# Half-width Fourier products, the full call's norms inside the context call, and a decay step without GpSimd, in a two-layer SSD, Fourier and mixture-of-experts block

## The reference, cut to what matters

```python
def _token_mixer(u, uc, ...):
    pc = uc @ w_in
    yc, s_f, s_b = _bidir_ssd(xsc, dtc, a, bmc, cmc, s0, s0)     # context first
    p = u @ w_in
    y, _, _ = _bidir_ssd(xs, dt, a, bm, cm, s_f, s_b)            # then the latents
    def merge(proj, z_, x_, y_):
        y_ = (y_ + x_ * d).reshape(b_, l_, D_INNER)
        ssm = _gated_rms_norm(y_, z_, norm_w) @ w_br_ssm
        four = _fourier_mix(proj[..., OFF_FOUR:OFF_GATE]) @ w_br_four
        gates = sigmoid(proj[..., OFF_GATE:])
        return (gates[..., :D] * ssm + gates[..., D:] * four) @ w_out

def _fourier_mix(t):            # 4 groups of 256 features, 256 tokens
    f = fft2(t.reshape(1, 256, 4, 256), axes=(1, 3), norm='ortho').real

def _ssd(...):                  # chunks of 128 tokens, 24 heads in 4 groups of 6
    seg = acum[:, :, :, None] - acum[:, :, None, :]
    lmat = exp(where(tri, seg, -inf))
    y_diag = einsum('bclsg,bclsgr,bcsgrp->bclgrp', scores, lmat, xdt)
```

## Time and profile before

| | |
|---|---|
| median of 3 runs | 2913.14 us (2911.34 to 2913.22) |
| the profiled execution: its own time, its span | 2910.98 us, 2909.1 us |
| busy: TensorE, VectorE, ScalarE, GpSimd | 2614.9, 996.8, 496.0, 345.5 us |
| calls 0 and 1 of the mixer end, experts of layer 0 | about 860 us, to about 1640 us |
| call 2 | 1684.7 to 1798 us |
| call 3 | 1798 to about 2190 us |
| experts of layer 1 | to the end |
| from the first to the last `y_products` of calls 0, 1, 3 | 71.87, 77.19, 77.20 us |

### The profile page before, as it was taken

One profiled execution on the slowest core, in us unless ns is written; L12 is line 12 of the kernel. 1 busy time (PEld: TensorE's weight loads), 2 busy tenths in 40 slices (PEclk: granted clock), 3 DMA queues, 4 the chain that ended last, 5 costly groups with the idle time before them and its releaser, 6 DMA issues. The chain is left out here.

```text
span 2909.1 us, 35099 instructions
## 1 busy us (share of the span) xinstructions
PE 2614.9 (90%) x11348; PEld 1644.3 (57%) x11348; DVE 996.8 (34%) x2285; ACT 496.0 (17%) x964; POOL 345.5 (12%) x448
## 2 busy tenths in 40 slices
PE   6999999999997899999999886999997799999994
PEld 4876788877884333433443374877786343343431
DVE  1334914528357111111111575342914411111114
ACT  1222311323221111111111022132211011111110
POOL 0001300003001111212111000000300211121110
PEclk8999999999999999999999987999998899999997
DMA  8762543435333999999999841763433599999993
GB/s 298 238 210 82 161 137 119 160 98 163 104 131 150 392 409 403 410 408 404 409 407 386 308 133 44 250 230 106 156 116 105 223 407 384 394 402 391 382 366 139
DMA packets 293117, 742.93 MB, mean 255 GB/s; under 512 B 33176, under 2 KB 207904, under 8 KB 238240
## 3 DMA queue, kind: packets, MB, share of 16 engines
q1 hardware_dynamic: 264672, 666.11, 60.7%
q0 software_dynamic: 28352, 75.56, 6.7%
HBM read 735.12 MB, written 52.58 MB: 271 GB/s over the span
## 5 line engine op out<-in xcount | busy, mean ns | idle before, releaser
L712 PE MATMUL psum<-arena 128*128 128x256 f32 x1984 | 452.0, 389 | 18.0 <-ACT arena L1167 12.1
L1070 PE MATMUL psum<-arena 128*64 128x512 f32 x1472 | 363.5, 639 | 77.5 <-DMA arena<-in_w 77.3
L712 PEld LDWEIGHTS psum<-arena 128*128 128x128 f32 x1984 | 384.2, 196 | 73.7 <-ACT arena L1167 13.1
L945 PE MATMUL psum<-arena 128*128 128x512 f32 x832 | 374.3, 594 | 0.0
L1913 DVE COPY arena<-psum 128x512 f32<-128x512 f32 x92 | 63.6, 691 | 614.4 <-PE psum L957 310.3
L1070 PEld LDWEIGHTS psum<-arena 128*64 128x64 f32 x1472 | 113.8, 145 | 261.0 <-issue 255.5
L945 PEld LDWEIGHTS psum<-arena 128*128 128x128 f32 x832 | 152.1, 192 | 154.4 <-issue 154.4
L1370 ACT ACTIVATE arena<-psum 128x512 f32<-128x512 f32 x92 | 55.0, 598 | 1053.1 <-PE psum L957 589.2
L720 PE MATMUL psum<-arena 128*128 128x256 f32 (+1 forms) x1088 | 229.6, 373 | 5.0 <-ACT arena L1167 5.0
L720 PEld LDWEIGHTS psum<-arena 128*128 128x128 f32 x1088 | 201.0, 196 | 31.3 <-ACT arena L1167 5.2
L957 PE MATMUL psum<-arena 128*128 128x512 f32 x416 | 197.3, 618 | 5.8 <-DVE arena L1727 3.6
(11 more groups left out here) (302 smaller groups left out, 2597.6 us busy)
## 6 DMA issues: line engine op xcount, KB each, us to landing
arena<-in_w SPq DMA_DIRECT2D x414, 1024.0 KB, 13.2
arena<-in_w_in SPq DMA_DIRECT2D x92, 1024.0 KB, 5.1
arena<-in_w_ada SPq DMA_DIRECT2D x32, 1024.0 KB, 7.6
arena<-results POOLq DMA_DIRECT2D x12, 2048.0 KB, 10.0
arena<-in_w_br_ssm SPq DMA_DIRECT2D x24, 768.0 KB, 4.4
arena<-in_w_ada SPq DMA_DIRECT2D x8, 2048.0 KB, 14.8
arena<-cumulated SPq DMA_DIRECT2D x36, 384.0 KB, 3.9
arena<-in_w_br_four SPq DMA_DIRECT2D x12, 1024.0 KB, 5.0
```

Source lines behind the costliest of these rows:

```text
L712: last = mm(o[:, a, :], w[:, k, a * P:(a + 1) * P], rhs[:, k, :], start=first and k == 0, stop=final and k == ks - 1, skip_group_check=True)
L945: last = mm(o.rearrange("p (a n) -> p a n", a=2), lhs(k), w[:, k, :, :], start=k == 0, stop=k == KD - 1)
L1070: last = mm(bank[0][c, :].rearrange("p (a n) -> p a n", a=2), xTe[0][:, k, c], w13[b][:, k, :, :], start=k == 0, stop=k == KD - 1)
```

## The change

`FH` is 129, `TH` is 127 and `AHEAD`, the call that is prepared early, is 3.

1. **Half-width Fourier products.** The inputs are real, so the spectrum's second half mirrors the first. `feature_dft` now has 258 columns (129 cosines, 127 sines between two zero columns) instead of 512, with four banks (3 to 6) instead of two. `token_dft` has, for each of two feature tiles, two products of 129 columns and two of 127 instead of four of 256, into bank 7 (bank 3 for the last group). VectorE's new `unfold` takes the place of ScalarE's copy: a copy of 4 columns, a copy of 254 and four additions or subtractions of 127, two of them written backwards. The rows of `w_br_four` come in the order that this leaves. `token_dft` of groups 1 and 2 waits for the `unfold` before it. The first feature product stands ahead of the waits for the states and the modulation.
2. **Norms of the full call among the context call's.** Call 3's norms are made in call 2, after slabs xbc 3 and 4, its transposes and copies after slabs 5 and 6, into buffers that call 2 leaves free. Call 2's state products move behind the four "four" slabs of call 3, four each.
3. **No GpSimd in the decay.** The forward segments are made by ScalarE: six `Relu` and six `Exp` of 128 by 128 with a bias column each. VectorE keeps the backward ones, and makes both multiplications and the addition; `weigh(it)` now stands after `tail(it - 1)` and `head(it)` before it.

```diff
-    dft = np.zeros((2, SEQ, 2 * SEQ), np.float32)
+    dft = np.zeros((2, SEQ, 2 * FH), np.float32)
+    dft[0, :, 0:FH] = np.cos(ang[:, 0:FH])
+    dft[0, :, FH + 1:2 * FH - 1] = np.sin(ang[:, 1:FH - 1])
+    dft[1, :, 0:FH] = np.cos(ang[:, 0:FH]) / SEQ
+    dft[1, :, FH:FH + TH] = np.sin(ang[:, 1:FH - 1]) / SEQ
...
+        uT_of, mT_of, lnx_of = [uT, uT, uT, mT], [mT, mT, mT, uT], [lnx, lnx, lnx, zs_row]
...
+                    if m != AHEAD:
+                        for t in range(NT):
+                            u_transposes(m, t)
...
                             channel_major("four", j, uT, KD)
                             late_ada("four", j)
+                            if m == AHEAD:
+                                state_products(m - 1, False, 4 * j, 4 * j + 4)
...
+                        if m == AHEAD - 1 and j >= 5 and j < 7:
+                            u_transposes(AHEAD, j - 5)
...
-                    if not full:
-                        state_products(0, 16)
...
                         def feature_dft(g):
-                            if g >= 1:
-                                pe.wait_ge(t_f1c.sem, t_f1c.at(m, g))
+                            if g >= 2:
+                                pe.wait_ge(t_f1c.sem, t_f1c.at(m, g - 1))
...
                         def token_dft(g):
                             pe.wait_ge(t_f1c.sem, t_f1c.at(m, g + 1))
-                            if g >= 1:
+                            if 1 <= g < GROUPS - 1:
                                 pe.wait_ge(t_f2c.sem, t_f2c.at(m, g))
+                            o = bank[7 if g < GROUPS - 1 else 3]
                             for a in range(2):
-                                for i, (t, part) in enumerate([(t, part) for t in range(NT) for part in range(2)]):
-                                    last = mm(bank[6][:, a * SEQ:(a + 1) * SEQ],
...
+                                for at, n, src, c0 in ((a * FH, FH, a, 0), (2 * FH + a * TH, TH, FH + a, FH)):
+                                    for t in range(NT):
+                                        last = mm(o[:, at:at + n], fA[:, g % 2, t, src:src + P], dft[:, 1, t, c0:c0 + n], start=t == 0, stop=t == 1)
...
+                        def decay(it):
+                            c, h0 = it // GROUPS, (it % GROUPS) * HPG
+                            f, v = seg[it % 2]
+                            act.wait_ge(t_rin[it % 2].sem, t_rin[it % 2].at(m, 32 * (it // 2 + 1)))
+                            for r in range(HPG):
+                                i_ = a_(f[:, r, :], f[:, r, :], ACT.Relu, scale=-1.0, bias=acu[:, c, h0 + r:h0 + r + 1])
+                            link(i_)
+                            act.wait_ge(t_seg.sem, t_seg.at(m, it + 1))
                             a_(v, v, ACT.Exp).then_inc(t_exp.sem, 1)
+                            for r in range(HPG):
+                                i_ = a_(f[:, r, :], f[:, r, :], ACT.Exp, scale=-1.0, bias=log_dt[:, c, h0 + r:h0 + r + 1])
+                            i_.then_inc(t_exp.sem, 1)
...
+                        if m == AHEAD - 1 and j >= 3 and j < 5:
+                            norm(lnx_of[AHEAD][:, j - 3, :], xres[:, TILES[CALLS[AHEAD][1]][j - 3], :], t_lnx.sem)
...
+                            f, v = seg[it % 2]
+                            sm = smask[it % 2]
+                            link(V.tensor_tensor(v, v, sm[:, 1, :].unsqueeze(1).to_broadcast([P, HPG, P]), ALU.mult))
+                            dve.wait_ge(t_exp.sem, t_exp.at(m, 2 * it + 2))
+                            link(V.tensor_tensor(f, f, sm[:, 0, :].unsqueeze(1).to_broadcast([P, HPG, P]), ALU.mult))
+                            V.tensor_tensor(f, f, v, ALU.add).then_inc(t_lm.sem, 1)
...
+                        def unfold(g):
+                            dve.wait_ge(t_f2.sem, t_f2.at(m, g + 1))
+                            o = bank[7 if g < GROUPS - 1 else 3]
+                            cos_ = o[:, 0:2 * FH].rearrange("p (a t) -> p a t", a=2)
+                            sin_ = o[:, 2 * FH:2 * FH + 2 * TH].rearrange("p (a t) -> p a t", a=2)
+                            V.tensor_copy(fO[:, 2 * g:2 * g + 2, 0:SEQ:P], cos_[:, :, 0:FH:P])
+                            half = ytmp[:, g % 2, 0:2 * TH].rearrange("p (a t) -> p a t", a=2)
+                            link(V.tensor_copy(half, sin_))
+                            for a in range(2):
+                                f_ = fO[:, 2 * g + a, :]
+                                V.tensor_tensor(f_[:, 1:P], cos_[:, a, 1:P], half[:, a, :], ALU.add if a else ALU.subtract)
+                                last = V.tensor_tensor(f_[:, SEQ - 1:P:-1], cos_[:, a, 1:P], half[:, a, :], ALU.subtract if a else ALU.add)
+                            last.then_inc(t_f2c.sem, 1)
...
+                        unfold(0)
+                        unfold(1)
                         head(0)
+                        unfold(2)
+                        unfold(3)
                         weigh(0)
-                        for it in range(8):
-                            if it:
-                                tail(it - 1)
-                            if it % 2 == 0 and it:
+                        for it in range(1, 8):
+                            head(it)
+                            tail(it - 1)
+                            if it % 2 == 0:
                                 merge_four(it // 2 - 1)
-                            if it < 7:
-                                head(it + 1)
-                                weigh(it + 1)
+                            weigh(it)
```

More of the change, by code:

```diff
@@ L102 @@
 LATE_CALLS = (0, 3)
+AHEAD = 3
 ON_PE = 6
@@ L775, in _ @@
                     last.then_inc(t_acp.sem, 1)
-                    def heads_product():
-                        for c in range(NT):
-                            mm(bank[2][0:32, c * P:(c + 1) * P], adt[:, c, 0:32], tri_le, start=True, stop=True)
-                            last = mm(bank[2][32:HALF, c * P:(c + 1) * P], adt[:, c, 16:48], tri_ge, start=True, stop=True)
-                        last.then_inc(t_ctm.sem, 1)
                     def scores_product(it):
@@ L838, in _ @@
                             pe.wait_ge(s_const, 48)
+                        feature_dft(0)
+                        pe.wait_ge(t_st.sem, t_st.all(m))
                         if m in LATE_CALLS:
                             pe.wait_ge(s_modc, 2 * l + 2)
[L841 removed]
+                        for g in range(1, GROUPS):
                             feature_dft(g)
[L843 to L844 removed]
+                            token_dft(g - 1)
                         token_dft(GROUPS - 1)
@@ L1228, in _ @@
                             conv_out(j - 3)
+                        if m == AHEAD - 1 and j >= 5 and j < 7:
+                            u_copies(AHEAD, j - 5)
                     conv_silu(nx - 1)
@@ L1453, in _ @@
                         continue
-                    if m > 2 and not (CALLS[m - 1][0] == l and CALLS[m - 1][2]):
-                        for t in range(NT):
-                            norm(lnx[:, t, :], xres[:, TILES[stream][t], :], t_lnx.sem)
+                    mT = mT_of[m]
                     def product(kind, j):
```

136 lines of the change are left out of this document (63 added, 73 removed).

## The result

| | before | after |
|---|---|---|
| median of the runs | 2913.18 us (4 runs, 2911.34 to 2915.96) | 2831.74 us (4 runs, 2827.71 to 2834.53) |
| profiled execution | 2910.98 us, span 2909.1 us | 2834.27 us, span 2832.4 us |
| ratio of after to before | | 0.9719, 95% interval 0.9702 to 0.9735 |
| mean granted clock of TensorE | | 0.958 |

The change takes 81.4 us off the median. It is made from TensorE's timeline of each profile: a stage lasts from the start of its first row to the start of the next stage's first row.

What follows compares the result with a forecast made beforehand. TensorE was busy for 90% of the span, DMA engines at 90% in the experts, so gains must come in the mixer. 2911.0 - 46.9 - 17.3 - 17.8 = 2829.0, plus 2.1 for the median: 2831 us, range 2819 to 2850.

Steps and rivals of the forecast that it cites:

- Fourier products: Fourier stage of calls 0, 1 and 3: half-width products bring it to 14.8 us a call, saving 46.9 us.
- 0.8 us for semaphores: Fourier stage: allowance added to 14.0 us of products, giving 14.8 us a call.
- The 48% that the prediction set against the 38%: Token products: trace rows of 128 columns cost 0.112 against 0.215 for 256, 48% less; the skill page's ratio gave 38%.
- the rival on weight loads: Fourier stage: each 128-column record waits for its weight load, 15.6 us more in all, 2847 us; chance 0.03.
- Decay stage: First to last y_products: idle GpSimd stops stretching VectorE's tail; 64.2, 72.4 and 72.4 us, saving 17.3 us.
- Calls 2 and 3: Cumulated products of call 2 to end of call 3's four slabs: 55.3 us instead of 73.15, saving 17.8 us.
- 35.8 us, the first partly at low clock; I keep that: Call 3's four slabs with their modulation products: old length kept, before adding 17.6 us of state products and 1.9 of transposes.
- At nothing: Items costed at zero: ScalarE's twelve short instructions a round, norms hidden on VectorE, GpSimd's 48 instructions leaving, smaller table loads.
- Decay stage stays: Decay stage stays with VectorE's or ScalarE's chain, gaining 5 us instead of 17: 2843 us; chance 0.14.
- Pace of `unfold`: Fourier stage runs at the pace of VectorE's unfolding, 4.4 us a group, 18 a call: 2841 us; chance 0.08.
- State products dearer among the slabs: Call 3's slabs: waits for VectorE or low clock leave only 9 of the 17.8 us: 2840 us; chance 0.10.
- Clock: Fourier and decay stages: TensorE's clock falls to 1.2 GHz, 6.9 us more a round, up to 2997 us; chance 0.02.

Runs made afterwards that it cites:

- merge_last: The changed kernel with merge_four placed behind weigh instead of ahead of it: 2827.16 us, and 2829.24 us when repeated.
- gpsimd_busy: The changed kernel with GpSimd making an unneeded multiplication and addition of 768 columns on its own scratch in each decay round: 2880.4 us.
- norms_only: The kernel before with only call 3's norms and transposes moved into call 2 and call 2's state products among call 3's four slabs: 2892.98 us.
- scalar_more: The changed kernel with six more Relu of 128 columns into an unused buffer on ScalarE in every decay round: 2833.52 us.
- states_back: The changed kernel with call 2's sixteen state products in one block at its end again, norms and transposes still early: 2835.82 us.

## Why the prediction held, and where it was off

**Fourier products** (-46.9 forecast, -48.3 measured, 0.45 a call better). The token records at 0.112 were right, from the earlier trace rows. The 0.8 us for semaphores isn't there, since four banks leave no hand-over in the open; instead the four feature products take 7.06 where 4 x 1.72 = 6.9 were forecast, and the four token products 7.29 where 4 x 1.79 = 7.2 were. The ratio of the Trainium skill, "TensorE: Matmul & The Clock Gate", section "Back-to-back issue gap" (81 ns for 128 columns, 131 for 512), is one for a quarter of the columns, 38% less. The trace has 0.112 against 0.43 to 0.46 for 512 columns of float32, about 75% less. The 48% that the prediction set against the 38% is for half the columns (0.112 against 0.215), so the two were not alike, and the trace is further from the ratio than the prediction said. The row decided, and the rival on weight loads is refuted with it.

**Decay stage** (-17.3 forecast). First to last y_products were forecast at 64.2, 72.4 and 72.4 and came at 63.65, 73.07 and 73.06: 16.5, and 1.3 more ahead of the first, which the sum did not have. The mechanism is as forecast: 0.56 for each of the tail's instructions without GpSimd, which the kernel with a busy GpSimd confirms, and TensorE alone setting call 0, busy for 63.65 of 63.65. Merge rounds are 10.97 instead of 10.8; plain ones 10.06 instead of 10.0.

**Calls 2 and 3** (-17.8 forecast, -16.5 measured). The length without the transposes came at 54.9 against 53.4. The step that was off is the "35.8 us, the first partly at low clock; I keep that": it holds one slab at low clock, 9.17, while the rows show two, 9.96 and 8.52, and the slabs with their modulation products take 37.5. The 16 state products take 3.71, 3.69, 5.11 and 4.88 by fours, 17.4 against 17.6, but that agreement is luck: by the prediction's own prices (0.65, and 1.05 or 1.52) four of them are 3.4 or 4.3 and not 3.9 or 4.9, 15.5 in all. More important, the term gave no price to the two edits apart. Its reason, that state products under slabs cost less than in a block, is worth 1.2 us by one profile and no more than 5; the early norms are worth 15.2.

**At nothing**: ScalarE, the norms' own time and GpSimd's empty queue showed no cost. With everything, the stages save 82.6, the medians 81.4, and the spans of the profiled pair only 76.7. The difference is work that the change doesn't touch, and three stretches of the profiled pair hold nearly all of it. From call 0's last y_products to call 1's Fourier stage it is 274.72 before and 271.51 after, 3.2 saved, by the clock (see the last section). From call 1's last y_products to the end of call 2 (the start of its last cumulated products) it is 1028.87 and 1035.68, of which 1.75 are the transposes: 5.1 lost. From the last y_products of call 3 to the end of the last instruction on TensorE it is 787.06 and 791.48: 4.4 lost. The last of these is spread, since among five profiles of the changed kernel or of `merge_last` it is 787.3 to 791.5. The second is not only spread: it is 1028.7 to 1031.0 in the four profiles that lack a part of the change and 1034.1 to 1038.9 in the ten that have all three. Most of this stretch is the experts of layer 0, and there TensorE waits 48.1 us for weights at L1089, 43.5 at the same instruction before (L1070): that holds most of the 5.1. Why the experts wait longer behind a faster mixer stays open.

The agreement of 2831 with 2831.74 is thus better than the terms deserve, and part of it is luck: 1.4 too little for the Fourier products, 0.5 for the decay stage and 1.3 too much for calls 2 and 3 partly cancel, and so do the 3.2 between calls 0 and 1 and the 5 in the experts, neither of which the prediction had. Against the profiled execution, in which its sum was made, the forecast of 2829.0 was 5.3 too low (2834.27).

**The rivals.** Decay stage stays: refuted by 73.07 against 77.19. Pace of `unfold`: refuted, with no margin left. State products dearer among the slabs: half true, in that the low clock takes back what the spreading gives. Clock: not in the change's Fourier and decay stages (granted clock 1.00), but present as soon as GpSimd makes TensorE wait 3 us. The reason given against it, that a round follows a wait of 1.91 without such a loss, was a reading of one round (696.04): the rounds at 718.40 and 2083.25 of the same profile follow a wait of 1.91 too, and their four records of 384 columns took 2.88 and 2.73 instead of 1.51.

## What to carry to other kernels

Before moving an elementwise step to GpSimd, look at which VectorE instructions run beside it: those with both inputs in SBUF stretched here from 558 to 900 and 1300 ns, 14.8 us in call 1's stage, more than the 13.4 (14 instructions at 0.96) for which VectorE does GpSimd's share itself; those with an input in PSUM did not stretch. Cost a stage by its rows and not by medians, and run the parts of a change alone. Totals that add up don't yet say that the parts are independent: here 3.0 us and 2.8 us of dependence cancelled, and only the stages showed them. A stage that loses 1 us alone shows a queue that another part empties. In an in-order queue put what nobody waits for (the merge) behind what the bounding engine waits for: 5.4 us for moving one line.

## What the runs showed of the hardware

- In an otherwise dense stage the three waits of 3.00 us on TensorE (`gpsimd_busy`) were followed by records at the lower clock level (2.82 or 2.83 against 1.55), waits of 0.94 and 1.70 were not. Waits of about 2 us went either way: 1.91 without a fall at 696.04 and with one at 718.40 of the kernel before, and 2.11 with one in `norms_only` (2.75 against 1.55).
- The low clock after a thin stretch is paid by whatever comes next: 9.96 instead of 7.07 by a slab, probably little by state products that VectorE paces.
- The same wait does not always cost clock: ahead of call 0's output products ScalarE holds TensorE for 1.4 us in both kernels, and only in the first of these two rows, of before, were the twelve records slow; the second is of after. Such dips move untouched code: the stretch from call 0's last y_products to call 1's Fourier stage takes 271.4 to 272.6 in seven profiles and 274.1 to 276.4 in the seven others. It goes with the kernel: the three profiles of the changed kernel and the two of `merge_last` are all among the first seven, and so are `scalar_more` and `states_back`. What decides stays open.

```profile
388.10 4.54 PE L901 MATMUL psum<-arena 128*128 128x256 f32 x12 [1.40 <-ACT arena L1293]
```

```profile
361.85 2.86 PE L920 MATMUL psum<-arena 128*128 128x256 f32 x12 [1.41 <-ACT arena L1325]
```

- Writing a VectorE result backwards along the free axis costs nothing: 0.28 us for 127 columns, 0.29 forwards.
